# Sample attention: both sequences of a pair turned block by block, with the four score products of a block side by side

## What is computed

```python
s_c = jnp.einsum('bqghd,bngd->bghqn', qg, kc.astype(f32))
p_c = masked_softmax(s_c, c_end[None, :] <= q_pos[:, None])
o_c = jnp.einsum('bghqn,bngd->bqghd', p_c, vc.astype(f32))
imp = jnp.einsum('bghqn,ns->bgqs', p_c, sel_map)
_, idx = lax.top_k(imp, n_sel)
s_s = jnp.einsum('bqghd,bgqkd->bghqk', qg, g_kv[..., 0, :])
p_s = masked_softmax(s_s, (k_pos <= q_pos[:, None])[:, :, None])
o_s = jnp.einsum('bghqk,bgqkd->bqghd', p_s, g_kv[..., 1, :])
s_w = jnp.einsum('bqghd,bkgd->bghqk', qg, win_kv[:, :, 0].astype(f32))
```

## Time and profile before

| | us |
|---|---|
| median of the three executions | 2069.86 |
| span of the profiled execution, first to last instruction | 2065.7 |
| TensorE busy in that span | 1969.3 |
| VectorE, ScalarE, GpSimd busy | 1217.0, 615.1, 663.4 |
| sample attention, of the span | about 110 |

### The profile page before, as it was taken

One profiled execution on the slowest core, in us unless ns is written; L12 is line 12 of the kernel. 1 busy time (PEld: TensorE's weight loads), 2 busy tenths in 40 slices (PEclk: granted clock), 3 DMA queues, 4 the chain that ended last, 5 costly groups with the idle time before them and its releaser, 6 DMA issues.

```text
span 2065.7 us, 39742 instructions
## 1 busy us (share of the span) xinstructions
PE 1969.3 (95%) x15956; PEld 1237.7 (60%) x15956; DVE 1217.0 (59%) x2486; ACT 615.1 (30%) x1428; POOL 663.4 (32%) x774
## 2 busy tenths in 40 slices
PE   8999999988888998999988999999999999999999
PEld 6445656788886874455544545556656564747473
DVE  5375564366665548676655447856565655656473
ACT  5004543233433226666644222101010101101020
POOL 3000000244433002212203004556565656555561
PEclk9999999999999998999999999999999999999999
DMA  7000112200014811000036601111111111111112
GB/s 228 1 0 21 31 31 80 90 4 22 7 25 125 218 31 57 11 6 6 6 123 205 208 2 41 41 41 41 41 41 42 41 41 41 41 41 41 41 41 87
DMA packets 96661, 115.90 MB, mean 56 GB/s; under 512 B 32252, under 2 KB 68029, under 8 KB 96415
## 3 DMA queue, kind: packets, MB, share of 16 engines
q1 hardware_dynamic: 90718, 101.82, 15.8%
q10 hardware_dynamic: 3840, 6.29, 1.1%
q0 software_dynamic: 1920, 5.25, 0.8%
HBM read 104.75 MB, written 12.64 MB: 57 GB/s over the span
## 4 chain that ended last, share of the span: by engine, by line
PE 85%; DVE 9%; issue 3%; ACT 2%; DMA 1%; SPq 1%; POOL 0%; DVEq 0%; POOLq 0%; ACTq 0%
PE psum L1605 45%; PE psum L1608 33%; PE psum L2234 2%; PE psum L2116 2%; PE psum L2291 1%; DVE arena L2949 1%; DVE arena L3121 1%; DVE arena L3092 1%; DVE arena L2975 1%; ACT arena L1460 1%; DVE arena L3081 1%; SPq L874 0%; PE psum L1953 0%; DVE arena L3094 0%; DMA arena<-in_w_in_dram 0%
## 5 line engine op out<-in xcount | busy, mean ns | idle before, releaser
L1605 PE MATMUL psum<-arena 64*64 64x64 f32 (+16 forms) x11020 | 1025.0, 299 | 51.2 <-issue 21.1
L1605 PEld LDWEIGHTS psum<-arena 64*64 64x64 f32 (+6 forms) x11020 | 593.8, 143 | 386.4 <-issue 228.0
L1608 PE MATMUL psum<-arena 128*128 128x272 f32 (+1 forms) x2464 | 753.1, 467 | 6.3 <-DVE arena L3121 5.4
L1608 PEld LDWEIGHTS psum<-arena 128*128 128x128 f32 x2464 | 459.5, 190 | 298.9 <-issue 216.2
L3143 DVE TENSOR_TENSOR arena<-arena,psum 128x512 f32<-128x512 f32 x224 | 153.9, 687 | 217.1 <-PE psum L1608 216.2
L3121 DVE TENSOR_TENSOR arena<-arena,psum 128x272 f32<-128x272 f32 x328 | 141.6, 434 | 99.8 <-PE psum L1608 97.1
L1567 ACT ACTIVATE arena<-psum 128x272 f32<-128x272 f32 x64 | 25.4, 397 | 544.8 <-PE psum L1608 544.8
L1031 POOL TENSOR_TENSOR arena<-arena 128x512 f32<-128x512 f32 x17 | 21.6, 1271 | 360.9 <-DVE arena L2783 360.9
L1104 POOL TENSOR_TENSOR arena<-arena 128x544 f32<-128x544 f32 x49 | 65.8, 1343 | 165.0 <-PE psum L1608 165.0
L1460 ACT ACTIVATE arena<-psum,arena 128x640 f32<-128x640 f32 (+7 forms) x128 | 89.0, 699 | 52.1 <-DVE arena L2949 51.9
L1025 POOL TENSOR_TENSOR arena<-arena 128x256 f32<-128x256 f32 x82 | 61.5, 751 | 117.4 <-PE psum L1605 117.2
(11 more groups left out here) (327 smaller groups left out, 2015.1 us busy)
## 6 DMA issues: line engine op xcount, KB each, us to landing
arena<-in_w_up_dram SPq DMA_DIRECT2D x7, 2048.0 KB, 8.5
arena<-in_w_down_dram SPq DMA_DIRECT2D x7, 2048.0 KB, 7.8
arena<-in_cache_slc_kv_dram SPq DMA_DIRECT2D x96, 128.0 KB, 2.6
arena<-in_cache_cmp_kv_dram SPq DMA_DIRECT2D x72, 128.0 KB, 3.9
arena<-in_x_prompt_dram SPq DMA_DIRECT2D x16, 512.0 KB, 13.7
arena<-in_w_in_dram SPq DMA_DIRECT2D x13, 512.0 KB, 3.8
arena<-in_cache_cmp_kv_dram ACTq DMA_DIRECT2D x48, 128.0 KB, 3.7
arena<-in_w_in_dram SPq DMA_DIRECT2D x2, 2048.0 KB, 18.6
```

Source lines behind the costliest of these rows:

```text
L1605: return nc.tensor.matmul(out, lhsT, rhs, start=start, stop=stop)
L1608: return nc.tensor.matmul(out, lhsT, rhs, start=start, stop=stop, skip_group_check=True)
```

## The change

In the front, the eight steps are taken in another order: block q of sequence 2p, block q of sequence 2p+1, then block q+1 of both. The scores of a block are issued for both sequences in one run of four products, after the turns of the next block. The wait for a sequence's pages stays before its first turn, which is now at j = 0 for the first and j = 1 for the second sequence. The scores of the window blocks are issued as four products after the second window block is copied. The semaphore for the slots counts as before, one for each sequence's two products.

```diff
-            def s_scores(p_, j):
-                bb, q = divmod(j, 4)
-                pe.wait_ge(sem("sg_out"), group_no["k", p_, j] + 1)
-                if j == 0 and p_ >= 1:
+            def s_scores(p_, q):
+                pe.wait_ge(sem("sg_out"), group_no["k", p_, 2 * q + 1] + 1)
+                if q == 0 and p_ >= 1:
                     pe.wait_ge(sem("ss_add"), 5 * p_)
-                if j == 0 and backs_ahead("front", p_) > 0:
+                if q == 0 and backs_ahead("front", p_) > 0:
                     pe.wait_ge(sem("sa_out"), backs_ahead("front", p_))
-                for b, g, r in quads(p_)[2 * bb:2 * bb + 2]:
-                    ins = mm(banks[q][r, :], sq_of(b, g), kt_r[kslot["k", p_, j] % 4][HALVES[g], :])
-                ins.then_inc(sem("sg_k"), 1)
+                for b, g, r in quads(p_):
+                    keys = kt_r[kslot["k", p_, 2 * q + b % 2] % 4]
+                    ins = mm(banks[q][r, :], sq_of(b, g), keys[HALVES[g], :])
+                    if g == KVH - 1:
+                        ins.then_inc(sem("sg_k"), 1)
...
                 for j in range(8):
-                    bb, q = divmod(j, 4)
+                    q, bb = divmod(j, 2)
                     b = 2 * p_ + bb
...
                     s_turn("k", p_, j, *[page_at(b, 4 * q + x)[:, 0, :] for x in range(4)])
-                    if j >= 1:
-                        s_scores(p_, j - 1)
+                    if bb == 1 and q >= 1:
+                        s_scores(p_, q - 1)
...
-                s_scores(p_, 7)
+                s_scores(p_, 3)
...
-                for bb in range(2):
-                    pe.wait_ge(sem("sg_out"), group_no["w", p_, bb] + 1)
-                    for b, g, r in quads(p_)[2 * bb:2 * bb + 2]:
-                        ins = mm(banks[7][r, :], sq_of(b, g), kt_r[kslot["w", p_, bb] % 4][HALVES[g], :])
-                    ins.then_inc(sem("sg_k"), 1)
+                pe.wait_ge(sem("sg_out"), group_no["w", p_, 1] + 1)
+                for b, g, r in quads(p_):
+                    ins = mm(banks[7][r, :], sq_of(b, g), kt_r[kslot["w", p_, b % 2] % 4][HALVES[g], :])
+                    if g == KVH - 1:
+                        ins.then_inc(sem("sg_k"), 1)
```

## The result

Over 20 executions of each, the changed kernel takes 2073.05 us (median) and the kernel before 2069.82: a ratio of 1.002, with a 95% interval of 1.0012 to 1.0029, so 2.5 to 6.0 us slower. That is inside the range and inside what I had called no change, but my sum said 0.27 us. The profiled execution of the changed kernel took 2068.62 us, its span 2066.9: only 1.7 us lie around a span, not the 4.2 I took. With 1.7 the profiled execution before took about 2067.4 us.

A forecast was written before the change was run, and what follows sets the result against it. TensorE bounds a front, by about 2 us only, with VectorE's ranking behind it. Early gains are waited off at the second turn: 0.15 + 0.2 - 0.08 = +0.27 us, 2070.1 us against 2069.86; range 2066 to 2074.5.

The forecast's parts named there:

- A run of four costs 1.05 us.: Front blocks: four products take 1.05 us, 0.99 plus 0.06 for two weight loads; a block falls from 3.14 to 2.2 us.
- The slower rival: Fronts 1 and 3 and windows: four products do not run at once, 1.98 us a run, 9.3 us more, 2079.4 us; 4%.
- Front 0 wins 2.0 us, bounded by VectorE's ranking.: End of front 0: masking starts at about 1059.13, not 1061.13, so front 1's first products start at 1061.75; 2.0 us gained.
- Fronts 1 and 3 wait for pages at the second turn, and give the gain back.: Second turns wait until 1067.45 and 1121.95; 11.1 us on, back 0 begins 0.15 us later, back 2 0.08 us earlier.
- pages in time: Rival, second sequence's pages are there in time at the second turn: 5.3 us won, 2064.8 us; 4%.
- pages later still: Rival, pages of sequences 3 and 7 land one us later each, competing with the window's load: 2072 us; 10%.
- the clock stays up: Rival, full clock around the late second turn: 1.2 us saved in each of fronts 1 and 3, 2067.7 us; 12%.
- Front 2 wins some 2 us, and front 3 gives them back.: Front 2 gains some 2 us by the ranking's bound; front 3 waits for sequence 7's pages, back 2 at 1133.05.
- The window's four products cost 0.05 us a back.: Window scores: the first two products now wait for the second copy; 0.05 us for each of four backs, 0.2 us.
- The backs, the projection's loads behind them and the MLP move with it.: Everything behind the fronts was said to shift along with them; no separate term in the sum.
- The 4.2 us around the span: Time outside the profiled span, added to the forecast span of 2066.0 us to give 2070.1 us.
- the sum of +0.27: Whole kernel: 0.15 (front 1) + 0.2 (windows) - 0.08 (front 3) = +0.27 us, giving 2070.1 against 2069.86.

The follow-up runs named there:

- the kernel with pairs: The changed order of turns, early wait included, with the products still issued in twos, against the kernel before: 2075.71 us, ratio 1.0049 (1.0031 to 1.0066).
- the kernel with the window part alone: The kernel before with only the window scores issued as four products; fronts in the old order: 2066.35 us, ratio 0.9994 (0.9981 to 1.0006).
- idle products in the fronts alone: The changed kernel plus 128x512 products nobody reads before the second turn's page wait in fronts 1 to 3: 2068.92 us, ratio to before 1.0003.
- the 35.65 us at a clock of 1.00: The changed kernel plus two 128x512 products nobody reads at the hand-over to the output projection: 2068.71 us, ratio to before 1.0009 (0.9998 to 1.002).
- the kernel with halves: The changed kernel with the second pair's pages loaded four by turns and TensorE waiting per half sequence: 2064.94 us, ratio to before 0.9983.
- the kernel with the wait alone: The kernel before plus only a wait for the second sequence's pages before a front's second turn: 2077.61 us, ratio 1.005 (1.0031 to 1.007).

## Why the prediction was right, and where it was not

- *A run of four costs 1.05 us.* Right: 1.06 us in front 0. By the Trainium skill ("TensorE: Matmul & The Clock Gate", section "Part 3: Packing small matmuls — row/col tiling") a weight load overlaps only where the row group differs, and the run would take 1.98; the trace disagrees, for four products on two row halves and four column groups. The slower rival falls with the 1.06 us, and the kernel with pairs shows what the four are worth: 4.8 us.
- *Front 0 wins 2.0 us, bounded by VectorE's ranking.* Nearly: 1.58. The idle time before line 3029 is gone, but the ranking itself came later. With nothing to do ahead of the softmax TensorE idled 2.01 us and lost its clock (0.50 granted from 1050 to 1053 us, where it was 1.00 before), so head sum and transpose reached VectorE's copy 1050.84 - 1049.80 = 1.04 us after they began, and not 1050.86 - 1050.22 = 0.64. The 0.40 is the difference. I had named the emptied wait and not its clock.
- *Fronts 1 and 3 wait for pages at the second turn, and give the gain back.* Right: counted from the first turn of front 0, released by the DMA at 20.45 (forecast 1067.45 - 1047.12 = 20.33) and 74.96 (74.83). The path from there to back 0 took 10.53 us (11.1), to back 2 10.58. The rivals "pages in time" and "pages later still" fall on these lines, and "the clock stays up" on the turns of 1.11 us. The eighth turn waited 1.15 us for ScalarE, behind the exponential, as forecast.
- *Front 2 wins some 2 us, and front 3 gives them back.* The win failed, though the two traces seem to confirm it. Sequence 5 was there by 1104.2 as I bounded it (its turn starts at 1103.12), but TensorE still waited 1.62 us for it, and 2.7 to 3.0 in three other traces of the new order; so my bound, a stall at fronts 1 and 3 only, was wrong. The 1.99 us come from the kernel before having lost as much in its traced execution; against the kernel with the window part alone it is 0.3 us lost. The sum does not hang on it, because the pages of sequence 7 set where back 2 begins: forecast at 1133.05 - 1047.12 = 85.93, measured 85.54. It hangs on what this is set against, and that was one late execution: 86.02, where the window part alone has 83.79.
- *The window's four products cost 0.05 us a back.* Right within what can be told: 0.13 us for backs 2 and 3 together.
- *"The backs, the projection's loads behind them and the MLP move with it."* This is the step that failed, and it stood in the sum at nothing. The backs did (22.89 us against 22.76) and the MLP did (873.1). The hand-over did not: 2.13 us more than in the trace I read, 1.33 more than with the window part alone. All five traced kernels with four products side by side and none of the idle products have 38.7 to 38.9 us there, the five with pairs in the fronts 35.6 to 37.9. With idle products in the fronts alone it is 37.3. That it is the clock, the 35.65 us at a clock of 1.00 show, and the order of the 14 traces. Why what a front does should be felt in the clock of the hand-over, two backs and 23 us later, the runs do not say.
- *The 4.2 us around the span* were 1.7. The number came from setting one execution's span against the median of others.

So the sum of +0.27 went wrong in two places. Within the attention it held against the trace that it was read from (0.35 us earlier measured), but that execution had ended the attention 1.6 us later than the mean of the three traces of the old order; and the hand-over cost 2.2 us by the means, where the sum had nothing. With both, -0.35 + 1.6 + 2.2 makes 3.5 us, where 3.2 (2.5 to 6.0) were measured. The forecast of under 2 us either way failed by that; the range and the chance of no change beyond 0.3% held.

## What to carry to other kernels

When a change lets TensorE issue the same work in less time, look at what fills the waits it had been covering, and price the clock behind each new gap as well as the gap. A wait that moves forward in the order takes its loads' order with it: move both, as the kernel with halves did, and the same change wins. Landmarks counted from the stage's start, in traces of two kernels that share the disputed part, show what one execution's luck was.

## What the runs showed of the hardware

Four products of 64 x 32 weights and 512 columns, two on each half of the rows, each with 32 columns of its own, ran in the time of two (1.06 and 1.05 us). The lower clock cost about as much as the idle time that it went with: in the kernel with the wait alone, 2.28 us of waiting made front 1 longer by 4.54 us than before. The hand-over took 35.6 to 35.8 us at a granted clock of 1.00 and 38.7 to 38.9 where it was 0.50 from 2 to 6 us behind its start. Measured side by side, the mean granted clock over the executions was 0.9825 for the changed kernel and 0.9880 before; products whose results nothing reads raised it to 0.9865 and were worth 2.6 us by the medians, with intervals that overlap. The Trainium skill ("TensorE: Matmul & The Clock Gate", section "HAM oscillation — how this bites in real kernels") tells of a kernel whose TensorE waits for a DMA before each group of products and starts each group at the lower clock; the turns of fronts 1 and 3 agree (1.11 and 1.12 us after the wait, 0.65 without).
